# A hybrid decoder layer on one core: q, k, v, z order of the delta stage's projections, and two accumulators for the long convolution

## The reference, cut to what matters

```python
proj = x @ w_in                                  # q, k, v, z, decay, beta, GLU, two gates
qkv = silu(causal_depthwise_conv(qkv, conv_qkv)) # 4 taps
q, k = l2norm(q), l2norm(k)                      # per head of 128 channels
o = gated_delta_rule(q, k, v, g, beta)           # 8 heads, a state of 128x128 each
o = rmsnorm(o) * o_norm_g * silu(z)
branch_a = o @ w_oa
u = glu[..., :C] * sigmoid(glu[..., C:])
u = causal_depthwise_conv(u, dw_w) + dw_b        # 31 taps
u = silu(layer_norm(u)); branch_b = u @ w_ob
h = (sigmoid(gate_a) * branch_a + sigmoid(gate_b) * branch_b) @ w_o
```

## Time and profile before

| what | value |
|---|---|
| median of 3 runs | 2600.63 us (2599.25 to 2603.05) |
| the profiled execution's own time | 2599.02 us |
| its span | 2597.4 us |
| mean granted TensorE clock | 0.967 |
| start of the delta stage, to the first solve's L684 | 51.5 to 198.84 us |
| its 16 solves, to the end of the last one's work | 198.84 to about 1132 us |
| TensorE busy over the span | 92% |
| VectorE busy over the span | 68% |
| ScalarE, GpSimd | 51%, 26% |

### The profile page before, as it was taken

How to read it: one execution, slowest core, us unless ns; L and a number is a source line. 1 busy time by engine, 2 the same in 40 slices (tenths; PEclk the granted TensorE clock), 3 DMA queues, 4 the chain that set the end, 5 groups by cost and what they waited for, 6 DMA issues and landing times. The chain is left out here.

```text
span 2597.4 us, 40492 instructions
## 1 busy us (share of the span) xinstructions
PE 2379.9 (92%) x11611; PEld 1936.0 (75%) x11612; DVE 1770.7 (68%) x2279; ACT 1324.2 (51%) x1723; POOL 688.0 (26%) x674
## 2 busy tenths in 40 slices
PE   7989998999999899958999796899999998999995
PEld 6868777777777788846778575688888887888782
DVE  3347888888888866637855485577767786677645
ACT  3254565456556444424522132577767776667640
POOL 2002121112212111112101312444444443444430
PEclk9989999999999999988999898899999999999998
DMA  4434543322333354344565235899999999999935
GB/s 118 74 45 72 63 56 65 83 58 58 74 66 51 66 97 106 82 170 134 185 199 190 90 81 177 267 280 326 307 277 309 323 327 344 285 289 292 330 79 216
DMA packets 244141, 435.91 MB, mean 168 GB/s; under 512 B 25096, under 2 KB 149000, under 8 KB 244046
## 3 DMA queue, kind: packets, MB, share of 16 engines
q1 hardware_dynamic: 211198, 350.70, 46.4%
q0 software_dynamic: 32848, 83.96, 12.4%
HBM read 370.88 MB, written 97.71 MB: 180 GB/s over the span
## 5 line engine op out<-in xcount | busy, mean ns | idle before, releaser
L59 PE MATMUL dn_pj<-x_hi,dn_hi 128*128 128x512 f32 x1024 | 432.4, 422 | 1.8 <-PEq L84 1.8
L61 PE MATMUL dn_pj<-x_hi,dn_lo 128*128 128x512 f32 x1024 | 404.4, 395 | 0.0
L60 PE MATMUL dn_pj<-x_lo,dn_hi 128*128 128x512 f32 x1024 | 402.2, 393 | 0.0
L1079 DVE SCALAR_TENSOR_TENSOR uc_half<-u_in,par,uc_half 128x512 f32<-128x512 f32 x480 | 380.0, 792 | 12.7
L59 PE MATMUL gu_ps<-e_hi,xg_hi 128*128 (+1 forms) x752 | 311.9, 415 | 0.0
L2572 DVE TENSOR_TENSOR e_lo<-e_raw,e_hi (+1 forms) x128 | 292.5, 2286 | 20.7 <-ACT e_hi L2511 20.7
L61 PE MATMUL gu_ps<-e_hi,xg_lo 128*128 (+1 forms) x752 | 296.2, 394 | 0.0
L60 PE MATMUL gu_ps<-e_lo,xg_hi 128*128 (+1 forms) x752 | 295.0, 392 | 0.0
L2511 ACT ACTIVATE e_hi<-e_raw (+1 forms) x128 | 245.1, 1916 | 43.3 <-PEq L84 35.2
L61 PEld LDWEIGHTS dn_pj<-x_hi,dn_lo 128*128 128x128 f32 x1024 | 193.9, 189 | 44.5
L59 PEld LDWEIGHTS dn_pj<-x_hi,dn_hi 128*128 128x128 f32 x1024 | 194.8, 190 | 34.0 <-issue 2.9
(11 more groups left out here) (390 smaller groups left out, 4931.7 us busy)
## 6 DMA issues: line engine op xcount, KB each, us to landing
e_raw<-in_w_gate_e_dram SPq DMA_DIRECT2D x128, 512.0 KB, 5.7
e_raw<-in_w_up_e_dram SPq DMA_DIRECT2D x128, 512.0 KB, 8.0
e_raw<-in_w_down_e_dram SPq DMA_DIRECT2D x128, 512.0 KB, 8.0
dn_raw<-in_w_in_dram SPq DMA_DIRECT2D x64, 512.0 KB, 7.9
gate_rows<-qkv_next SPq DMA_DIRECT2D x16, 512.0 KB, 2.6
br_raw<-in_w_oa_dram SPq DMA_DIRECT2D x16, 512.0 KB, 4.9
br_gate<-gate_rows SPq DMA_DIRECT2D x32, 256.0 KB, 4.5
br_raw<-in_w_ob_dram SPq DMA_DIRECT2D x16, 512.0 KB, 4.1
```

What stands on the lines that cost most here:

```text
L59: nc.tensor.matmul(out, w_hi, x_hi, start=first, stop=False)
L60: nc.tensor.matmul(out, w_hi, x_lo, start=False, stop=False)
L61: return nc.tensor.matmul(out, w_lo, x_hi, start=False, stop=last)
L1079: ins = stt(out=uc[:], in0=u_in[:, t:t + HALF], scalar=w, in1=uc[:], op0=ALU.mult, op1=ALU.add)
```

## The change: what it does

`KIND` becomes (0, 1, 2, 3): step 0 projects q, step 1 k, step 2 v, step 3 z. With it move the norms (sums, Ln and Exp, scales) from solves 2 and 3 to 1 and 2, the short convolutions from steps 1 to 3 to steps 0 to 2, the copies `cur_k` and `cur_q` to level 3 of solve 3, and the Silu of v to level 2 of solve 3. The convolution of a step's second head is split: its first two taps before level 1 of the next solve, the other two in level 1. z's store goes from POOL's solve 1 to solve 0. TensorE's one fill step ahead of L684 in solve 0 goes behind L686. The taps alternate between `uc` (even) and a new `uc2` (odd, named uc_odd), taps 0 and 1 are plain multiplies, and a 32nd instruction adds uc2 and the bias to `uc`. `tap_plan` is new, with `first` taps before level 1 and `late` taps after the second right side (5 where 2 stood).

```diff
-            KIND = (3, 0, 1, 2)
+            KIND = (0, 1, 2, 3)
...
-                return G * 6 + 2 * (p - 1) + j
+                return G * 6 + 2 * p + j
...
                     if p == 0:
-                        f(1)
                         pe.wait_ge(cur_ready, g * 2 + 2)
...
-                    if p > 0:
-                        f(1)
+                    f(1)
...
-                        if more and p in (2, 3) and l <= 4:
+                        if more and p in (1, 2) and l <= 4:
...
                         if p == 0:
-                            tile_silu(g, 3, 1)
                             glu_move(g, 3)
...
                         if more and l == 2 and p > 0:
+                            if p == 3:
+                                tile_silu(G, 2, 0)
                             tile_silu(G, p - 1, 1)
-                        if more and p in (2, 3) and l <= 4:
+                        if more and p in (1, 2) and l <= 4:
                             norm(G, p - 1, l - 1)
...
-                        if more and l == 6 and p == 3:
+                        if more and l == 3 and p == 3:
                             cur_k(G)
...
-                        if more and cc == 1:
+                        if more and cc == 1 and p < 2:
                             tile_silu(G, p, 0)
...
-                        tap_plan = ((5, 5, 5, 4, 3, 4), (6, 5, 3, 2, 5, 5), (7, 5, 3, 2, 2, 7), (7, 5, 3, 2, 2, 10))[p]
+                        first, tap_plan, late = ((3, (7, 3, 4, 1, 2, 5), 5), (2, (5, 5, 6, 2, 0, 5), 5),
+                                                 (2, (5, 5, 6, 2, 0, 5), 5), (2, (3, 3, 5, 5, 2, 5), 5))[p]
                     else:
-                        tap_plan = (5, 4, 5, 5, 5, 2)
+                        first, tap_plan, late = 2, (5, 4, 5, 5, 5, 2), 2
...
+                            acc = uc2 if t % 2 else uc
...
-                                ins = v.tensor_scalar(uc[:], u_in[:, 0:HALF], w,
-                                                      self.par[:, bass.ds(g * 2 + p // 2, 1), R_DWB],
-                                                      ALU.mult, ALU.add)
+                            if t < 2:
+                                ins = v.tensor_scalar(acc[:], u_in[:, t:t + HALF], w, None, ALU.mult)
                             else:
-                                dve.wait_ge(taps_done, 1 + q * TAPS_L + t)
-                                ins = stt(out=uc[:], in0=u_in[:, t:t + HALF], scalar=w, in1=uc[:],
+                                dve.wait_ge(taps_done, 1 + q * SUMS + t - 1)
+                                ins = stt(out=acc[:], in0=u_in[:, t:t + HALF], scalar=w, in1=acc[:],
                                           op0=ALU.mult, op1=ALU.add)
                             ins.then_inc(taps_done, 1)
+                            if t == TAPS_L - 1:
+                                dve.wait_ge(taps_done, 1 + q * SUMS + TAPS_L)
+                                stt(out=uc[:], in0=uc2[:], scalar=self.par[:, bass.ds(g * 2 + p // 2, 1), R_DWB],
+                                    in1=uc[:], op0=ALU.add, op1=ALU.add).then_inc(taps_done, 1)
...
                     if more and p > 0:
-                        conv(G, p - 1, 1)
+                        conv(G, p - 1, 1, range(0, 2))
...
-                        if more and p in (2, 3) and l == 5:
+                        if more and p in (1, 2) and l == 5:
                             for m in range(4):
                                 scale(G, p - 1, m)
+                        if more and l == 1 and p > 0:
+                            conv(G, p - 1, 1, range(2, TAPS_S))
                         taps(tap_plan[l - 1])
+                        if more and l == 3 and p == 3:
+                            cur_q(G)
...
+                        elif l == 5 and more:
+                            k_beta(q + 1, G, 0)
...
                         if cc == 0:
-                            taps(early)
+                            taps(1)
                             right_side(1)
-                        if cc == 0 and more and p == 3:
-                            cur_q(G)
-                            k_beta(q + 1, G, 0)
-                            conv(G, p, 1, range(0, 1))
-                        elif cc == 0:
-                            taps(3 - early)
+                            taps(late)
                             dve.wait_ge(s_upd, 1 + q * 2 + 1)
...
-                    if more and p == 3:
-                        conv(G, p, 1, range(1, TAPS_S))
...
-                    if more and p == 1:
-                        z_store(g + 1)
+                    if p == 0:
+                        z_store(g)
...
-                    pool.wait_ge(taps_done, 1 + q * TAPS_L + TAPS_L)
+                    pool.wait_ge(taps_done, 1 + q * SUMS + SUMS)
```

More of the change, by code:

```diff
@@ L435, in delta_net @@
             kd, vb = (sb(ctx, n, [P, 4, P]) for n in ("k_dec", "v_beta"))
+            uc2 = sb(ctx, "uc_odd", [P, HALF])
+            SUMS = TAPS_L + 1
             st = sb(ctx, "state", [P, GH, P])
@@ L640, in norm_sum @@
                 def norm_sum(G, p, m):
-                    pe.wait_ge(sq_done, G * 4 + 2 * (p - 1) + m // 2 + 1)
-                    after(pe, rn_done, G * 8 + 4 * (p - 1) + m)
+                    pe.wait_ge(sq_done, G * 4 + 2 * p + m // 2 + 1)
+                    after(pe, rn_done, G * 8 + 4 * p + m)
                     mm(gd[:].rearrange(FLAT), self.ones[:],
@@ L670, in k_state @@
                             pe.wait_ge(act_ln, 1 + q)
-                        if cc == 0 and more and p in (2, 3):
-                            pe.wait_ge(rn_done, G * 8 + 4 * (p - 1))
+                        if cc == 0 and more and p in (1, 2):
+                            pe.wait_ge(rn_done, G * 8 + 4 * p)
                         if cc == 0 and p == 0:
@@ L786, in _ @@
                                 fill(tile_no(0, p, i), k)
-                    if p >= 2:
+                    if p in (1, 2):
                         for m in range(4):
@@ L811, in tile_move @@
                     ps = pj[n % 2][:].rearrange(FLAT)
-                    if p == 0:
-                        after(act, n_scaled, G * 8)
+                    if p == 3:
+                        act.wait_ge(n_scaled, G * 8 + 8)
                         A(zt[j][:], ps, ACT.Silu).then_inc(pj_moved, 1)
@@ L845, in tile_silu @@
                     act.wait_ge(conv_sem, (c + 1) * 2 * TAPS_S)
-                    if p == 3:
+                    if p == 2:
                         act.wait_ge(kvt_done, 1 + G * 4)
-                    dst = cur if p == 3 else nxt
+                    dst = cur if p == 2 else nxt
                     A(dst[:, KIND[p], j, :], nxt[:, KIND[p], j, :], ACT.Silu).then_inc(silu_done, 1)
-                    if p < 3:
+                    if p < 2:
                         act.wait_ge(silu_done, c + 1)
-                        if p == 1:
-                            act.wait_ge(z_stored, G * 32 + 32)
+                        if p == 0:
+                            after(act, z_stored, G * 32)
                         else:
@@ L858, in norm @@
                 def norm(G, p, m):
-                    i = G * 8 + 4 * (p - 1) + m
+                    i = G * 8 + 4 * p + m
                     act.wait_ge(ns_done, i + 1)
@@ L865, in norm_exp @@
                 def norm_exp(G, p):
-                    act.wait_ge(rn_done, G * 8 + 4 * p)
+                    act.wait_ge(rn_done, G * 8 + 4 * p + 4)
                     for j in range(2):
@@ L973, in _ @@
                     for j in range(2):
-                        if (p, j) != (3, 1):
-                            tile_silu(0, p, j)
+                        tile_silu(0, p, j)
                     if p < 3:
                         glu_move(0, p)
-                tile_silu(0, 3, 1)
                 cur_k(0)
@@ L1002, in conv @@
                         if p == 1 and j == 0:
+                            after(dve, k_tail, G)
+                        if p == 0 and j == 0:
                             after(dve, cur_ready, G * 2)
-                        if p == 3:
+                        if p == 2:
                             after(dve, silu_done, G * 6)
@@ L1026, in scale @@
                 def scale(G, p, m):
-                    dve.wait_ge(rn_exp, G * 4 + 2 * (p - 1) + m // 2 + 1)
+                    dve.wait_ge(rn_exp, G * 4 + 2 * p + m // 2 + 1)
                     half = slice(m % 2 * HALF, (m % 2 + 1) * HALF)
@@ L1105, in solve @@
                     tt(qk[:], gb[:], dt[:], ALU.mult).then_inc(self.qk_sem, 1)
-                    taps(2)
+                    taps(first)
                     if p > 0:
@@ L1155, in solve @@
                             k_beta(q + 1, g, p + 1)
-                    early = 0 if more and p == 3 else 1
+                        elif l == 5 and more:
+                            k_beta(q + 1, G, 0)
                     for cc in range(2):
@@ L1202, in z_store @@
                     for j in range(2):
```

(2 more changed lines are left out.)

8 lines of the change are left out of this document (5 added, 3 removed).

## The result

| | before | changed |
|---|---|---|
| median | 2600.59 us (2599.25 to 2603.05, 4 runs) | **2569.27 us** (2566.55 to 2570.64, 4 runs) |
| profiled execution, its span | 2599.02, 2597.4 us | 2566.55, 2565.0 us |
| start of the stage, to the first solve | 198.84 us | 203.14 us |
| first solve to the start of the last one | 864.87 us | 828.20 us |
| VectorE busy over the span | 68% | 68% |

The ratio is 0.9871, 95% interval 0.9856 to 0.9885: 31 us faster. The two spans differ by 32.4 us, and two rows of the table close the sum: the solves give 36.7, the start takes 4.3 back, and nothing behind the solves changes by more than 0.1. (Lines shift with the change: L684 is now L685, L676 is L678, L1104 is L1111, and so on.)

The account below looks back on a forecast made before the run. PE was taken to bound the kernel, busy 55.7 of 61.5 us in g2p3. Gains of 44.7 less losses of 11.0, net 33.7, took 2599.0 to 2565.3; 1.6 more for the median gave 2567, range 2554 to 2589.

Parts of the forecast that it names:

- Silu of v: Head of solve p = 0: with v's Silu gone from there, PE's three waits at L697 vanish, 7.7 us gained.
- VectorE's waits: First three groups: PE's waits for VectorE at L676, L762, L720 and L717 all go, with restarts 32.2 us gained.
- Thin margin in level 4: Level 4 of p = 1 and 2: VectorE's work fits by only 0.4 us; 0.2 in each of six solves, 1.2 lost.
- The clock: g0p3, g1p3, g3p0: falls of PE's clock behind waits of 2.6 us and more go, 3 x 1.6 = 4.8 us gained.
- Norms unchanged: Norm sums, Ln, Exp and the waits at L644 and level 5's L746 move to p = 1, 2 unchanged: 0.
- The seam: Between solves: five taps and the add delay POOL's decay, so PE waits at L705, at twelve seams, 7.2 us lost.
- Silu's new place: Level 2 of p = 3: two Silus more on ScalarE make PE wait at L746, 3 x 0.87 = 2.6 us lost.
- At nothing: Moves priced at zero, among them the start's norm sums one step earlier, with q and k ready sooner than wanted.
- A: Rival: the seam and v's Silu in its new place cost nothing, 2557 us; chance 0.12.
- C: Rival: taps still start 0.79 us apart, costing 11 in six solves and 8 at twelve seams, 2586 us; chance 0.06.
- D: Rival: uc's store lands late and holds VectorE's queue at the seams, slower, 2640 us if 12 us were the rule; chance 0.05.
- E: Rival: ScalarE truly ends most waits put down to VectorE, so they pass to others, 2595 us; chance 0.03.

Follow-up runs that it names:

- run 6: Changed kernel with the second Silu of v back at the head of the group, the first left in level 2 of p = 3: 2582.52 us.
- Run 4: Kernel before with taps on two accumulators and the closing add, old order and old tap numbers kept: 2590.58 us.
- run 3: Changed kernel with the taps on one accumulator again, no closing add, new order and tap numbers kept: 2572.58 us.
- Run 9: Kernel before with five of the ten taps ahead of the first state update in p = 3 moved behind the second right side: 2605.6 us.
- run 7: Changed kernel with each tap waiting for the tap just before it, two accumulators and closing add kept: 2581.04 us.
- run 2: Changed kernel with the decay's two POOL operations moved ahead of the store of uc: 2562.41 us.
- run 1: Changed kernel with the first solve's gc and beta loads issued on SyncE ahead of the start's last three weight tiles: 2560.56 us.

## Why the prediction was right, and where by luck

The time came out 2 us from the forecast, and in part by luck: the solves from g0p1 on gained 6.1 us more than forecast, and the start with the first solve lost 7.4 that stood nowhere. By the terms:

*Silu of v:* 7.7 forecast; the waits at L697 are gone, and run 6, which brings one Silu back, loses 13.2. **Right.**

*VectorE's waits:* 32.2 forecast; the three kinds are gone from the first three groups, as said. **Right in the sum, and open in the reason.** The prediction divided the cause between the even load and the shorter taps without saying which decides. Run 4 gives the accumulators alone 10 us, run 3 takes them from the changed kernel for 3.3: the order and the new tap numbers, without the accumulators, bring 28 of the 31. Run 9 shows that one new placing of the taps without the order brings nothing; order and tap numbers were not parted further.

*Thin margin in level 4:* 1.2 lost was forecast. The margin is that thin: in six solves level 5's L720 starts 2.14 us behind level 4's L746 and not 1.84, too little for the list, and in run 7 the slower taps bring a wait of 1.6 there. But the 0.3 us cost nothing, for PE then waits that much less at level 5's L746: **0**.

*The clock:* 4.8 was forecast; g0p3 and g1p3 gave 1.6 each. So did g3p0: it fell by 3.0 (63.91 to 60.90) though a fill step of 1.4 came into it, 4.4 together, of which the wait and its restart are 2.8. **4.8, right.**

*Norms unchanged:* the L746 wait of level 5 fell from 1.22 to 0.82 in six solves. That is no gain: ScalarE's y_pairs end 6.1 us behind the last norm sum's start in both kernels, and from level 4's L746 to level 5's it is 5.30 us in both.

*The seam:* 7.2 lost forecast, the mechanism down to POOL's queue; 3.4 and eleven restarts, **5.3**, came, and run 2 won 6.9 by undoing it. In g2p2 L705 starts 8.1 us behind L685 (748.84 less 740.75), just as forecast, and 0.45 later than before. The prediction took these 0.45 for the wait alone and added a restart; the delay holds both (0.28 and 0.17), and the seams with a wait are eleven, not twelve. *Silu's new place:* 2.6 forecast, three waits of 0.22 came, **1.2**.

Together the solves from g0p1 on gained 39.8 us, not 33.7. The terms as measured (7.7, 32.2 and 4.8 less 5.3 and 1.2) make 38.2 of it; the other 1.6 are not put down to a term here.

*At nothing:* the step that failed. "In the start of the stage the two groups of norm sums come one step earlier and stall PE as before, and q and k are ready for the first solve sooner than PE wants them." Both halves hold: PE's stalls there are 10.1 us in both kernels, and q and k were ready at 191. But k_beta takes the beta rows too, and these hang on a queue whose release is PE's progress. Moving the norm sums took away the cover behind which the rows landed: start +4.3, g0p0 +3.1, **7.4 lost** where nothing was forecast. (The fill step of 1.4 us that went from the start into g0p0 is in both numbers and cancels; the 7.4 are the wait of 5.7 and the clock's 2.9, less 1.2 that g0p0 gained otherwise.)

**The rivals.** A (the seam and Silu's place cost nothing) did not come: they cost 5.3 and 1.2. B did not come. C, taps at 0.79, did not come, and was priced at 19; run 7, with 0.78, is that case and costs 11.8 (13.9 over the solves from g0p1 on). The price of level 4 was right for the wait (1.6 and a restart) and too high for the sum, since a part of the wait replaces the one of level 5 behind it. The rule of the Trainium skill named there, page "VectorE: DVE Perf Modes", section "The DRAIN you can't avoid", that a semaphore between chained operations costs nothing extra, does not hold in run 7: waiting for the tap directly ahead costs 0.12 us a tap more than waiting for the one before it. D, the store landing late, did not come: tap 0 waited for the store 5.1 us in all, in two of sixteen solves, on VectorE, and PE never for that. E falls, for the waits that were put down to VectorE are gone from the list.

## What to carry to other kernels

When work is moved from one place to another, ask what landed behind it: a stall can be the cover of a load, and a load that waits in a queue for PE's progress is issued later against PE when the stall goes. Price a wait together with the next one on the same engine, for it can take that one's place: 1.6 us at L720 took 0.8 from the wait at L746 (run 3). When a late engine is relieved, it may be that only the work behind the last point at which it still had to wait counts; that is how I read run 4, and no run isolates it. A semaphore wait for the operation directly ahead costs VectorE 0.12 us here beside a wait for the one before it; two interleaved chains avoid that, and it pays if the closing add does not stand on the way to the next step.

## What the runs showed of the hardware

- **Distance of a wait.** Multiply-adds of 128x512 in fp32 with the same operands start 0.66 us apart when each waits for the one before last, 0.78 when it waits for the last (run 7, against the changed kernel).
- **The clock's price varies for one and the same wait.** Behind the 5.66 us wait at L685 the solve g0p0 took 2.9 us more than without it (run 1); behind 5.3 and 5.5 us at the same place in runs 3 and 7 only 1.5 and 1.4 (49.96 and 49.87 against 48.44). Of the three state waits of 3.4 us in the kernel before, two cost 1.6 and one nothing, and the wait of 2.6 at L697 in g3p0 cost 1.6, while five of 2.3 at the same place (two in the kernel before, three in run 4) left the solve at 1.00; in run 4 one of 3.12 cost 2.7 (58.40 us of PE's work, granted clock 0.95, against 55.67). A wait up to 1.6 us never brought a granted clock below 1.00 in a solve's window read here. What decides between 0 and 2.9 stays open.
- **Rows that go to all partitions land slowly.** gc and beta, 256 KB each, landed 6.0 and 11.3 us behind their issue at the start, and 8.0 and 11.1 in the median of sixteen; conv_rows, as large, 2.8. At the start they stand directly behind a weight tile of 512 KB, and no run parts the kind of transfer from its place behind that tile.
- **Table loads between Ln and Exp.** ScalarE loads a table of 1.28 us ahead of the Ln and one ahead of the Exp in each norm and each output (L878 and L880, L862 and L868); they stand ahead of the copies for which PE waits at L746. The Trainium skill, page "ScalarE: Activation LUTs", section "Table sets: the hidden batching unit", lists a set that holds both functions, by which one load would do. No run here tried it.
